# Inversion of the triangular blocks on compact 64x64 tiles in the quarters of the array, and the decode states two heads at a time

## What is computed

```python
def step(s, inp):                       # for every token, every head
    r_t, w_t, k_t, v_t, kk_t, a_t = inp
    sa = jnp.einsum('bhvk,bhk->bhv', s, -kk_t)
    s = s * w_t[:, :, None, :] + sa[..., None] * (kk_t * a_t)[:, :, None, :] + v_t[..., None] * k_t[:, :, None, :]
    return s, jnp.einsum('bhvk,bhk->bhv', s, r_t)
s_fin, o = lax.scan(step, s0, ...)      # prompt: from zero; sample: from state_rwkv, 8 sequences
```

## Time and profile before

| | us |
|---|---|
| median of 3 runs | 1867.42 (1865.56 to 1868.09) |
| the profiled execution, its span | 1866.6 |
| RWKV phase, first DVE instruction of tile 0 to the end of the sample tile's fills | 314.5 to about 1308 |
| a prompt tile in the loop | 105.6 |
| PE busy over the span | 1578.3 (85%) |
| DVE / ACT / POOL busy | 864.3 / 480.3 / 383.9 |
| mean granted clock of TensorE | 0.902 |

### The profile page before, as it was taken

How to read it: one execution, slowest core, us unless ns; L and a number is a source line. 1 busy time by engine, 2 the same in 40 slices (tenths; PEclk the granted TensorE clock), 3 DMA queues, 4 the chain that set the end, 5 groups by cost and what they waited for, 6 DMA issues and landing times. The chain is left out here.

```text
span 1866.6 us, 27124 instructions
## 1 busy us (share of the span) xinstructions
PE 1578.3 (85%) x11156; PEld 1436.3 (77%) x11156; DVE 864.3 (46%) x1441; ACT 480.3 (26%) x819; POOL 383.9 (21%) x257
## 2 busy tenths in 40 slices
PE   4999997999989999998999999999222726899798
PEld 4899997898989888898989889956111614899686
DVE  5180002547465465546455464333589724444132
ACT  5122111314132222313232232300102125333221
POOL 4111222202020111202020110100256104333410
PEclk6999998999999999999999999965756868899899
DMA  5532422203030211203020211201761174344242
GB/s 157 125 100 87 132 82 93 70 20 95 24 91 10 78 42 45 71 23 91 28 76 25 58 52 31 64 21 32 269 96 15 39 134 163 118 125 139 99 145 79
DMA packets 164188, 151.41 MB, mean 81 GB/s; under 512 B 35615, under 2 KB 148688, under 8 KB 163488
## 3 DMA queue, kind: packets, MB, share of 16 engines
q1 hardware_dynamic: 164080, 149.79, 28.2%
HBM read 98.79 MB, written 49.79 MB: 80 GB/s over the span
## 5 line engine op out<-in xcount | busy, mean ns | idle before, releaser
L308 PE MATMUL f_ps<-h_hi,fw_hi 128*128 128x384 f32 (+1 forms) x864 | 305.5, 354 | 19.3 <-ACTq L660 12.7
L310 PE MATMUL f_ps<-h_hi,fw_lo 128*128 128x384 f32 (+1 forms) x864 | 287.2, 332 | 0.0
L309 PE MATMUL f_ps<-h_lo,fw_hi 128*128 128x384 f32 (+1 forms) x864 | 286.9, 332 | 0.0
L617 POOL TENSOR_TENSOR fw_lo<-fw,fw_hi 128x1024 fp32r<-128x1024 f32 x36 | 98.5, 2736 | 738.7 <-ACT fw_hi L657 738.7
L308 PEld LDWEIGHTS f_ps<-h_hi,fw_hi 128*128 128x128 f32 x864 | 166.6, 193 | 28.9 <-issue 17.5
L309 PEld LDWEIGHTS f_ps<-h_lo,fw_hi 128*128 128x128 f32 x864 | 166.7, 193 | 4.4 <-issue 4.4
L308 PE MATMUL proj_ps<-h_hi,whi 128*128 128x384 f32 (+1 forms) x504 | 165.6, 329 | 1.1 <-PEq L217 1.1
L310 PEld LDWEIGHTS f_ps<-h_hi,fw_lo 128*128 128x128 f32 x864 | 166.1, 192 | 0.0
L309 PE MATMUL proj_ps<-h_lo,whi 128*128 128x384 f32 (+1 forms) x504 | 165.4, 328 | 0.0
L310 PE MATMUL proj_ps<-h_hi,wlo 128*128 128x384 f32 (+1 forms) x504 | 165.4, 328 | 0.0
L674 ACT ACTIVATE f_out<-f_ps 128x384 f32<-128x384 f32 (+1 forms) x108 | 51.0, 472 | 267.7 <-PE f_ps L310 267.6
(11 more groups left out here) (450 smaller groups left out, 3112.5 us busy)
## 6 DMA issues: line engine op xcount, KB each, us to landing
fw<-in_w_in_dram SPq DMA_DIRECT2D x36, 512.0 KB, 4.5
projected<-f_out SPq DMA_DIRECT2D x72, 192.0 KB, 1.9
up_gate<-projected SPq DMA_DIRECT2D x24, 544.0 KB, 3.7
projected<-proj_out SPq DMA_DIRECT2D x21, 544.5 KB, 3.6
wst<-in_w_in_dram SPq DMA_DIRECT2D x21, 512.0 KB, 5.1
raw<-projected SPq DMA_DIRECT2D x8, 838.5 KB, 6.8
projected<-f_out SPq DMA_DIRECT2D x36, 160.0 KB
up_y<-y_branches SPq DMA_DIRECT2D x8, 544.0 KB, 4.8
```

The source lines that it names most:

```text
L308: pe.matmul(out, whi, xhi, start=first, stop=False)
L309: pe.matmul(out, whi, xlo, start=False, stop=False)
L310: return pe.matmul(out, wlo, xhi, start=False, stop=last)
L617: pool.tensor_tensor(wlo[:, r], wst[:, r], whi[:, r].bitcast(F32), ALU.subtract).then_inc(fw_lo, 1)
```

## The change

For the prompt tiles and the sample tile:

- The A matrix, T and X are stored compactly as `[P, 4, 2, C]`: two heads (even, odd) and 64 columns for each of four head pairs b, 512 numbers per partition in place of 1024. The matmuls X and TX become 64x64x64: 16 for 8 heads and 2 chunks, in the four quarters of the array (rows by the operand's half, columns by the output's), with different row halves writing to different PSUM banks. The transposes of T take two heads in one 128x128 instruction, 4 in place of 8 per level, and there is one more set ahead of level 0 and after the last one in place of the set that turned the first T.
- A second product set (alpha, beta) gives T's start directly, so the 8 transposes of L1013 and their copies go; it adds 16 quarter matmuls. DVE makes T's start in 3 instructions of 128x512, and masks the other products in 6 instructions of 64x512 in place of 12 of 64x256.
- The masks of X and the subtractions on DVE and the copies of T on ACT are 128x256 in place of 128x512.
- After the last level T is turned and laid out into `t_f` for GU: 4 transposes on PE, 2 copies on ACT and 2 on DVE, waited for by GU (`tf_sb`).
- The hardware loop over the tiles on PE, ACT, DVE and POOL is written out.
- Setup: level masks of 64 columns, each made by 4 selects in place of 2, an identity `id_st` of two halves; the turned states are stored by two DMAs of half the partitions.

For the sample tile's states: heads go in pairs, the odd head in the upper 64 partitions. B and K are stacked in one operand of 128 rows (`kbm`), U and V likewise (`vt`), so that one matmul gives both terms. PE waits for the evacuation of the pair before (`sn_sb`) ahead of a pair's new state, because the accumulators are no longer double. POOL clears `rpm` (`s_ad`, `s_bd`, `sample_spare`) after the outputs of prompt tile 7. Each transfer of states is 256 KB.

The core of the diff:

```diff
-        ab_t, ak_t, rb_t, rk_t = (sb(n, [P, H, P]) for n in ("ab_t", "ak_t", "rb_t", "rk_t"))
-        t_m, t_t, x_m = sb("t_m", [P, H, P]), sb("t_t", [P, H, P]), sb("x_m", [P, H, P])
+        ak_t, rb_t, rk_t, t_f = (sb(n, [P, H, P]) for n in ("ak_t", "rb_t", "rk_t", "t_f"))
+        ab_c, t_m, t_p, x_m = (sb(n, [P, 4, 2, C]) for n in ("ab_c", "t_m", "t_p", "x_m"))
+        spare = sb("sample_spare", [P, 4, 4, C])
...
+    products(beta, alpha, 0, 0)
+    products(alpha, beta, 0, 1).then_inc(ev["prod_mm"], 1)
...
+    def x_products(q):
+        for b in (2 * q, 2 * q + 1):
+            for par in (0, 1):
+                for c in t.halves:
+                    rows = slice(C * c, C * c + C)
+                    mm = mm_(qs[HD * par:HD * par + HD, 2 * q + c, (b % 2) * C:(b % 2) * C + C], ab_c[rows, b, par, :], t_m[rows, b, par, :],
+                             start=True, stop=True)
+        mm.then_inc(ev["x_mm"], 1)
+    if n:
+        for q in range(2):
+            pe.wait_ge(ev["tx_sb"], level_at(t, n - 1, q))
+            x_products(q)
+            turn_t(n, q)
...
+    for q in range(2):
+        pe.wait_ge(ev["x_sb"], level_at(t, n, q))
+        pe.wait_ge(ev["tt_sb"], level_at(t, n, q))
+        for b in (2 * q, 2 * q + 1):
+            for par in (0, 1):
+                rows = slice(HD * par, HD * par + HD)
+                for c in t.halves:
+                    mm = mm_(qs[C * c:C * c + C, 2 * q + par, (b % 2) * C:(b % 2) * C + C], t_p[rows, b, c, :], x_m[rows, b, c, :], start=True, stop=True)
+        mm.then_inc(ev["tx_mm"], 1)
...
-                with pe.Fori(1, TILES) as i:
+                for i in range(1, TILES):
...
+                        for p in range(H // 2):
+                            r, two = p % 2, (0, 1)
+                            pe.wait_ge(ev["mask_sb"], 2 * p + 2)
+                            if p:
+                                pe.wait_ge(ev["mz_sb"], p)
+                            for par in two:
+                                mm = mm_(Q[1][HD * par:HD * par + HD, :], n_g[C:C + T, 2 * p + par, :], kbm[r][par][C:C + T], start=True, stop=True)
+                            mm.then_inc(ev["mz_mm"], 1)
+                            if p:
+                                pe.wait_ge(ev["sn_sb"], 2 * p)
+                            for par in two:
+                                mm_(Q[SNB[par]][HD * par:HD * par + HD, :], vt[:, 2 * p + par, :], kbm[r][par], start=True, stop=False, skip_group_check=True)
```

More of the change, by code:

```diff
@@ L530, in turn_at @@
         def turn_at(t, n, q):
[L532 to L539, removed]
@@ L628, in body @@
                     n_lo = [0]
+                    if not t.prompt:
+                        pool.wait_ge(ev["o_mm"], TILES)
+                        for z in (s_ad[:, :, :], s_bd[:, :, :], spare[:, :, :, :]):
+                            pool.memset(z, 0.0).then_inc(ev["zeroed"], 1)
                     def lo_next():
@@ L647, in body @@
                     lo_next()
-                with pool.Fori(0, TILES) as i:
+                for i in range(TILES):
                     body(Tile(e, i, True))
@@ L700, in body @@
                         d = ay[0:T, :, 0:HD] if dst is None else dst[0:T]
+                        if not t.prompt and dst is bCt:
+                            d = kCt[C:C + T]
                         act.activation(d, Q[bank][0:T, :].rearrange("p (h k) -> p h k", h=H), ACT.Copy).then_inc(ev["turned_sb"], 1)
                     evacuate("T")
[L703 to L706, removed]
+                    for n in range(t.levels):
                         evacuate(f"X{n}")
@@ L830, in body @@
                         for c in t.halves:
-                            for par in (0, 1):
-                                ins = tt(half(blk(dst, c), par), prod(n, par, C * c, C), mb(m, C * c, C), ALU.mult)
-                                if c == t.halves[-1] and par:
-                                    ins.then_inc(ev["prod_sb"], 1)
-                                else:
-                                    ch.after(ins)
+                            to = blk(dst, c) if t.prompt or dst is not rb_t else rk_t[C:C + T, :, 0:T]
@@ L838, in body @@
+                            ins = tt(half(to), prod(n, PROD[n][1], C * c, C), mb(m, C * c, C), ALU.mult)
+                            if c == t.halves[-1]:
+                                ins.then_inc(ev["prod_sb"], 1)
+                            else:
+                                ch.after(ins)
+                    nh = len(t.halves)
                     for n in range(t.levels):
[L839 removed]
                         for q in range(2):
                             dve.wait_ge(ev["x_mm"], level_at(t, n, q))
[L842 removed]
+                            tt(swap(pair(x_m, t, q)), qs[:, 2 * q:2 * q + nh, 0:128].rearrange("p c (b t) -> p c b t", b=2),
+                               e.lv[:, n:n + 1, :].rearrange("p o (u t) -> p o u t", u=1).to_broadcast((P, nh, 2, C)), ALU.mult).then_inc(ev["x_sb"], 1)
@@ L938, in _ @@
                 k = body(t0, 0)
-                with dve.Fori(1, TILES) as i:
+                for i in range(1, TILES):
                     t = Tile(e, i, True)
@@ new lines, in body, with turn_t @@
+                    pe.wait_ge(ev["turned_sb"], i * 4 + 4)
+                    settle(3)
+                    for n, (l, r_) in enumerate(((kappa, alpha), (kappa, rho), (beta, rho)), 1):
+                        products(l, r_, *PROD[n]).then_inc(ev["prod_mm"], 1)
+                    fill("T")
+                    def turn_t(n, q):
+                        bank, first = (TBANK, 0) if n == t.levels else (TBANK + q, 2 * q)
+                        for b in (2 * q, 2 * q + 1):
+                            at = (b - first) * T
+                            mm = pe.transpose(qs[:, bank, at:at + T], t_m[0:T, b].rearrange("p o s -> p (o s)"), e.ident[0:T, 0:T])
+                        mm.then_inc(ev["tt_mm"], 1)
```

305 lines of the change are left out of this document (149 added, 156 removed).

## The result

The changed kernel takes 1733.55 us (median of 4 runs, 1728.54 to 1740.95) against 1866.49 of the kernel before: a ratio of 0.9287, 95% interval 0.9271 to 0.9302. The prediction was 1727, in a range of 1705 to 1785. The profiled execution has a span of 1732.5 us, 134.1 less than before; its mean clock is 0.913. In two experiments (e7 and e9) one unchanged program has two groups of times, and both groups are given there.

What follows compares the result with a forecast made beforehand. PE's in-order instruction list was taken to bound the kernel; 79 us saved in eight prompt tiles, 59.5 in the sample's states and 1 in its other work make 139.5 off 1866.6, so 1727 us, range 1705 to 1785.

Runs made afterwards that it cites:

- e7: Kernel before, with POOL instead of DVE clearing the operands of the sample's states, behind G and U: four runs of 1823.9 to 1826.3 us, two of 1858.7 and 1860.6.
- e9: The program of e7 run once more, unchanged: one run of 1831.9 us and four of 1861.0 to 1868.2.
- e11: As e7, with the three pieces from behind the sample's heads put into heads 0, 1 and 3: two runs, 1831.11 and 1839.48 us.
- e4: Changed kernel with T turned by 64x64 identity products in quarters, order T0, X0, X1, T1, results in other banks: 1735.25 us.
- e6: Changed kernel with e4's turning of T and four more pieces moved ahead of the feature transposes: 1702.72 us, ratio 0.9121 to the kernel before.
- e8: As e6, with one piece from ahead of a tile's last transposes put between the outputs and the second new state: 1698.55 us.

## What to carry to other kernels

When a change makes an engine's list sparser, ask of every stretch beside it, too, whether the clock holds, and compare tiles of the same program at different clocks before crediting an edit with a microsecond. After a stage has become shorter, deal the filler work anew: here the table of pieces, untouched by the change, was worth 61 us with one new place in it, nearly half as much as the change itself. Try the new deal on the kernel before as well: here that wasn't done, and the wait that it removed, 35.2 us, was there already. A gain in a stage that ran at the low clock should be split, since a cheaper edit may bring the clock alone.

## What the runs showed of the hardware

- The stretches of low clock in a tile, 3.5 to 10.5 us long, lie at or behind a wait, a stop or a sparse part; tiles of the same instructions took 98.96 and 95.60 us for it.
- One program (e7) takes 1824 to 1826 or 1859 to 1861 us, at mean clocks of 0.920 to 0.927 or 0.900 to 0.909; its one-quarter list ran at 0.50 in the profiled execution. With three pieces of full-array work among the heads all eight ran at 1.00 (e11, one profile).
- Levels of quarter products alone had stops of PE of up to 2.05 us, each ending 2.3 to 3.2 us after a code packet started, and lost the clock only behind such stops (e4, e6, e8); those with two full-array transposes in each half had one such stop in all profiles, of 0.20 us, and kept 1.00.
- Writing a loop of seven tiles out took 7 code packets fewer and 3 us less.
